# Expert weights of a Mamba-MLA decoder: the gate-up loads move from SyncE's DMA queue to ScalarE's

## Chip, cores and metric

One core of one Trainium2 chip. The metric is the device time of one launch in microseconds (us). The kernel before took 1404.7 us, the median of three runs that went from 1397.98 to 1405.53 us.

## The reference, cut to what matters

The model is a trunk of two layers, one step on 256 prompt rows and 64 sample rows (320 rows of 1024 numbers, float32). Layer 0 mixes tokens with a state-space scan, layer 1 with latent attention. Each mixer is followed by a mixture of experts, and this is the part that the change touches:

```python
def hier_moe(x, router, router_bias, w_gate, w_up, w_down):
    ...
    # every row picks one group of 8 experts, then 2 experts in it; gate = their weights
    for g in range(MOE_GROUPS):
        hg = silu(einsum('nd,edf->nef', xt, w_gate[sl])) * einsum('nd,edf->nef', xt, w_up[sl])
        hg = hg * gate[:, sl, None]
        out = out + einsum('nef,efd->nd', hg, w_down[sl])
```

There are 32 experts in a layer. One expert has a gate and an up matrix of 1024 x 256 and a down matrix of 256 x 1024: 2 MB of gate-up weights and 1 MB of down weights, some 100 MB in a layer. All of it is read from HBM once per layer.

## The kernel before, in words

`expert_layer(layer, afterwards)` (line 827) is called twice, after the scan and after the attention. Experts are worked on in 16 **pairs** (j = 0 to 15; pair j is experts 2j and 2j+1). Each expert has 64 places for rows, so that a pair fills the 128 partitions. The loop over windows (`Fori(0, n_windows)`) runs once here: no expert has more than 64 rows.

**Slots.** The weights of six experts lie in SBUF at a time: `slot(i)` is slot i % 6, four of them in `ring` and two in `hi`. A slot holds gate-up weights (16 KB in each partition) and behind them down weights (8 KB in each partition). So the loads of pair j go where pair j-3 was.

**TensorE** (lines 1131 to 1143) runs `gate_up(j+1)`, then `turn_hidden(j)`, `turn(j+2)`, `down(j)`. `gate_up` (L1098, 32 matmuls) waits for its gate-up loads; it makes gate and up outputs of both experts and raises `gu_done`. `turn_hidden` and `turn` are transposes (L1110, L1083); `down` (L1125, 16 matmuls) waits for its down loads and raises `d_done`. `idle_work` (L1024) is a pair of matmuls whose output nobody reads.

**ScalarE** (lines 1187 to 1197) runs, for each j, `silu(j+1)` (L1178, waits for `gu_done` of j+2), `rows_in(j+2)` (L1172, four activations behind `turn(j+2)`, which `gate_up(j+2)` waits for) and `rows_out(j)` (L1184, behind `down(j)`). Before the change it issues no weight load.

**SyncE** issues all weight loads on its own DMA queue, in an order written out by hand. The first six experts are issued ahead of the loop. Experts 6 and 7 (pair 3) are issued in halves (L219) as pair 0 is used. Then `stream(sp, 4, PAIRS + 1)` (lines 978 to 988) does for each j: wait until `gate_up(j-3)` has read its slots, issue the gate-up loads of pair j (L211, two DMAs); wait until `down(j-4)` is done, issue the down loads of pair j-1 (L224, two DMAs). Within one queue a later DMA's packets stand behind an earlier one's.

**GpSimd** gathers the input rows of pair j+3 (L1222, an indirect DMA) and scatters the output rows of pair j (L1230), on a third queue.

In the profile the queues have numbers: q1 is SyncE's, q10 ScalarE's, q0 GpSimd's. ScalarE's queue is used before the change for three loads at the end of each expert layer alone (L1205), beside three of SyncE (L1008).

Of the kernel before, what the change touches and what calls it, by code (L numbers as in the profile page):

```python
# [53 lines left out]
PAIRS = EXPERTS // 2  # L54
# [87 lines left out]
def program(nc, a, o):  # L142
    ctx = ExitStack()
    with ctx:
# [64 lines left out]
        def load_gate_up(sp, layer, i, slot):  # L209

            sp.dma_start(slot[:, 0:2 * KD * FF],  # L211
                         a["experts"][layer * EXPERTS + i][:, 0:2 * KD * FF]).then_inc(gate_up_in[i % RING], 16)

        def load_half_gate_up(sp, layer, i, slot, half):

            def part(x):
                return x.rearrange("p (g k f) -> p g k f", g=2, k=KD)[:, :, half * KD // 2:(half + 1) * KD // 2, :]

            sp.dma_start(part(slot[:, 0:2 * KD * FF]),  # L219
                         part(a["experts"][layer * EXPERTS + i][:, 0:2 * KD * FF])).then_inc(gate_up_in[i % RING], 16)  # L220

        def load_down(sp, layer, i, slot):

            sp.dma_start(slot[:, 2 * KD * FF:WEXP],  # L224
                         a["experts"][layer * EXPERTS + i][:, 2 * KD * FF:WEXP]).then_inc(down_in[i % RING], 16)

        def first_expert(sp, layer, i, slot=None):

            slot = ring[:, i, :] if slot is None else slot
            load_gate_up(sp, layer, i, slot)  # L230
            load_down(sp, layer, i, slot)
# [595 lines left out]
        def expert_layer(layer, afterwards):  # L827


            with ExitStack() as st:  # L830
# [39 lines left out]
                def slot(i):  # L870
                    return ring[:, i % RING, :] if i % RING < 4 else hi[:, i % RING - 4, :]
# [24 lines left out]
                def load_windows(eng):  # L896
                    eng.wait_ge(windows_set, 1)
                    return eng.value_load(windows[0:1, 0:1], min_val=1, max_val=MAX_WINDOWS)

                def meet(eng, w):  # L900

                    eng.wait_ge(go, w + 1)
                    eng.sem_inc(passed, 1)
# [65 lines left out]
                @block.sync  # L969
                def _(sp):  # L970
                    for t in range(NT):
                        sp.wait_ge(norm_set, t + 1)
                        sp.dma_start(x_dram[OFF[t]:OFF[t] + ROWS[t], :], X[0:ROWS[t], t, :]).then_inc(x_out, 16)
                    for i in (4, 5):
                        first_expert(sp, layer, i, slot(i))
                    n_windows = sp.alloc_register(f"windows_sp{layer}")
                    with sp.Fori(0, n_windows) as w:
                        def stream(sp, first, last):

                            for j in range(first, last):  # L980
                                if j < PAIRS:
                                    sp.wait_ge(gu_done, j - 2)
                                    for i in (2 * j, 2 * j + 1):
                                        load_gate_up(sp, layer, i, slot(i))
                                if j > 3:
                                    sp.wait_ge(d_done, j - 3)
                                    for i in (2 * j - 2, 2 * j - 1):
                                        load_down(sp, layer, i, slot(i))

                        for half in range(2):  # L990
                            sp.wait_ge(gu_done if half else half_done, 1)
                            for i in (6, 7):
                                load_half_gate_up(sp, layer, i, slot(i), half)
                        with sp.If(w < 1):
                            sp.wait_ge(x_scaled, 1)
                            sp.dma_start(lnp[:, :, :], a["ln"][2 * layer + 1]).then_inc(ln_in, 16)
                        stream(sp, 4, PAIRS + 1)
                        sp.wait_ge(d_done, PAIRS)
                        found = load_windows(sp)
                        sp.reg_mov(n_windows, found)  # L1000
                        sp.sem_inc(arrived, 1)
                        meet(sp, w)
                        with sp.If(w + 1 < found):
                            for i in range(RING):
                                first_expert(sp, layer, i, slot(i))
                    for t in range(NT):
                        r, row = ROWS[t], TOK + OFF[t]
                        sp.dma_start(places[NT + t][0:r, :], y_dram[row:row + r, :]).then_inc(got_in[NT + t], 16)  # L1008
                    if afterwards:
                        for got in got_in:  # L1010
                            sp.wait_ge(got, 16)
                        afterwards(sp)
                    else:
                        for t in range(NT):
                            sp.wait_ge(norm_set, NT + t + 1)
                            sp.dma_start(o["y"][0:ROWS[t], t, :], X[0:ROWS[t], t, :]).then_inc(stored, 16)
                        sp.wait_ge(stored, 16 * NT)
# [139 lines left out]
                @block.scalar  # L1157
                def _(act):
                    columns_in(act, 0)
                    statistics(act, 0)  # L1160
                    act.activation(spare[:, :], eps[:, 0:1], ACT.Sigmoid)
                    for t in range(NT):
                        flipped_act(act, 0, t)
                    act.wait_ge(logit_done, 2)
                    act.activation(aff[:, 0:2, :], ps[:, LG[0], 0:64].rearrange("p (t e) -> p t e", t=2), ACT.Sigmoid)
                    act.wait_ge(logit_done, 3)
                    act.activation(aff[0:64, 2, :], ps[0:64, LG[2], 64:96], ACT.Sigmoid).then_inc(aff_done, 1)

                    def rows_in(j):
                        act.wait_ge(turned, 2 * j + 1)  # L1170
                        for k in range(EARLY):
                            ins = act.activation(xsT[:, j % 2, k, :], ps[:, TP[0], k * P:(k + 1) * P], ACT.Identity,  # L1172
                                                 bias=gb[:, 0, 1, k:k + 1], scale=gb[:, 0, 0, k:k + 1])
                        ins.then_inc(xs_act, 1)

                    def silu(j):
                        act.wait_ge(gu_done, j + 1)
                        act.activation(sg[:, j % 2, :], ps[:, GU[j % 2], 0:FF], ACT.Silu).then_inc(silu_done, 1)  # L1178

                    def rows_out(w, j):  # L1180
                        act.wait_ge(d_done, j + 1)
                        if j >= 2:
                            act.wait_ge(ys_out[j % 2], PER_WINDOW * w + 16 * (j // 2))
                        act.activation(ys[:, j % 2, 0:512], ps[:, YB[0], :], ACT.Copy).then_inc(y_act, 1)  # L1184

                    n_windows = act.alloc_register(f"windows_act{layer}")
                    with act.Fori(0, n_windows) as w:
                        act.activation(spare[:, :], eps[:, 0:1], ACT.Silu)
                        rows_in(0)
                        silu(0)  # L1190
                        rows_in(1)
                        for j in range(PAIRS):
                            if j + 1 < PAIRS:
                                silu(j + 1)
                            if j + 2 < PAIRS:
                                rows_in(j + 2)
                            rows_out(w, j)
                        act.reg_mov(n_windows, load_windows(act))
                        act.wait_ge(y_act, PAIRS)
                        act.sem_inc(arrived, 1)  # L1200
                        meet(act, w)

                    for t in range(NT):
                        r, row = ROWS[t], OFF[t]
                        act.dma_start(places[t][0:r, :], y_dram[row:row + r, :]).then_inc(got_in[t], 16)  # L1205
                    act.activation(spare[:, :], eps[:, 0:1], ACT.Sqrt)
                    if layer == 0:
                        columns_in(act, 1)
                    statistics(act, 1)
                    if layer == 0:  # L1210
                        for t in range(NT):
                            flipped_act(act, 1, t)
# [986 lines left out]
```

## Time and profile before

| | |
|---|---|
| median of the runs | 1404.7 us |
| the profiled execution's own time | 1403.22 us |
| its span, first to last instruction | 1401.5 us |
| mean granted TensorE clock | 0.87 of full speed |
| TensorE matmuls busy | 1204.4 us, 86% of the span |
| ScalarE busy | 223.4 us, 16% |
| DMA traffic | 309.33 MB, mean 221 GB/s |
| share of SyncE's queue | 293.32 MB in 39666 packets |

The profile is of one execution. A line such as `L1098 PE MATMUL` is a group of instructions of one source line; "x32" is how many. In the timeline the bracket at a line's end says how long the engine was idle before and what ended it. A DMA engine is one of 16 that all queues of the core share; a "packet" of the profile is what such an engine moves in one piece. "DMA share" is how busy the 16 engines were on average; it can read a little above 1 because neighbouring packets overlap.

### The profile page before, as it was taken

What the parts mean: (1) busy time and instruction counts of PE and PEld (TensorE: products, weight loads), DVE (VectorE), ACT (ScalarE), POOL (GpSimd) and SP (SyncE); (2) the same over time, 40 slices, a digit from 0 to 9 for tenths busy, and PEclk for the clock granted to TensorE, in tenths of its full rate; (3) what the DMA queues carried; (4) which work ended last, traced back from release to release, by engine and by line L of the source; (5) the groups of instructions that cost most, each with busy time, mean ns of one, the idle gap of its engine ahead of it and who ended that gap; (6) DMA issues with size and microseconds to landing.
All of it is one profiled execution on the core that took longest, in us unless ns stands there. A gap on an engine that the chain in (4) does not pass through costs nothing. (4 is left out here: it accounts for less than half of the span.)

```text
span 1401.5 us, 14254 instructions
## 1 busy us (share of the span) xinstructions
PE 1204.4 (86%) x5008; PEld 641.1 (46%) x5008; DVE 442.5 (32%) x1137; ACT 223.4 (16%) x521; POOL 158.7 (11%) x231
## 2 busy tenths in 40 slices
PE   6999966676999699989999884889989989998981
PEld 4777754555566333543333323455554543333330
DVE  0037755543433410451212116222210362121115
ACT  0101121211000200311211112132120311111112
POOL 0000002423000000011111100314000011111100
PEclk9999987665555799899999996899999889999996
DMA  5333450000242224669999957535620869999973
GB/s 225 127 127 126 190 229 21 1 31 1 90 145 94 109 90 180 246 229 415 421 423 424 424 240 302 172 114 162 230 106 15 344 238 408 424 424 422 425 311 123
DMA packets 51726, 309.33 MB, mean 221 GB/s; under 512 B 12818, under 2 KB 13714, under 8 KB 30290
## 3 DMA queue, kind: packets, MB, share of 16 engines
q1 hardware_dynamic: 39666, 293.32, 52.5%
q0 software_dynamic: 11264, 12.61, 2.7%
q10 hardware_dynamic: 736, 2.62, 0.6%
q8 instruction: 35, 0.57, 0.2%
q14 instruction: 25, 0.20, 0.0%
HBM read 300.61 MB, written 30.97 MB: 237 GB/s over the span
## 5 line engine op out<-in xcount | busy, mean ns | idle before, releaser
L1098 PE MATMUL ps<-ring,xsT 128*64 128x512 f32 x704 | 166.7, 628 | 22.5 <-DMA ring<-in_experts 18.0
L302 PE MATMUL ps<-XT,ring 128*128 128x320 f32 x640 | 174.6, 436 | 11.3 <-DMA ring<-in_w_in 11.3
L302 PEld LDWEIGHTS ps<-XT,ring 128*128 128x128 f32 x640 | 122.7, 192 | 62.7 <-issue 12.7
L1098 PEld LDWEIGHTS ps<-ring,xsT 128*64 128x64 f32 x704 | 56.8, 144 | 129.4 <-issue 122.9
L1420 DVE TENSOR_TENSOR work<-work,ps 128x256 f32<-128x256 f32 x32 | 13.4, 420 | 272.2 <-ACT work L1178 272.2
L822 PE MATMUL ps<-ring,zT 128*128 128x512 f32 (+1 forms) x192 | 87.8, 605 | 0.0
L1125 PE MATMUL ps<-ring,hT 128*64 128x512 f32 x352 | 80.4, 598 | 2.2 <-DVE hT L1425 1.7
L1098 PE MATMUL ps<-hi,xsT 128*64 128x512 f32 x320 | 74.2, 618 | 7.5 <-DMA hi<-in_experts 7.3
L1230 POOL DMA_INDIRECT y_dram<-ys,index x32 | 32.1, 1004 | 378.1 <-DVE ys L1431 367.1
L1222 POOL DMA_INDIRECT XT<-x_dram,index x32 | 32.7, 1023 | 357.6 <-DVE index L1366 325.8
L1024 PE MATMUL ps<-C 128*128 128x512 f32 x124 | 70.6, 688 | 0.0
L721 PE MATMUL ps<-ring,Bm 64*128 64x512 f32 x64 | 57.5, 1077 | 0.0
L1178 ACT ACTIVATE work<-ps 128x256 f32<-128x256 f32 x32 | 12.3, 385 | 279.0 <-PE ps L1098 279.0
L822 PEld LDWEIGHTS ps<-ring,zT 128*128 128x128 f32 (+1 forms) x192 | 30.5, 172 | 56.8 <-issue 56.6
L530 PE MATMUL ps<-seg,ring 128*64 128x128 f32 (+1 forms) x192 | 22.3, 356 | 39.1 <-DVE seg L589 39.1
L1172 ACT ACTIVATE xsT<-ps,gb 128x128 f32<-128x128 f32 x128 | 48.2, 457 | 45.5 <-PE ps L1083 45.5
L1275 DVE SCALAR_TENSOR_TENSOR X<-X,ps 128x1024 f32<-128x1024 f32 (+1 forms) x6 | 7.3, 1211 | 137.5 <-PEq L759 79.1
L1098 PEld LDWEIGHTS ps<-hi,xsT 128*64 128x64 f32 x320 | 24.5, 142 | 56.2 <-issue 56.2
L1431 DVE COPY ys<-ps 128x512 f32<-128x512 f32 x32 | 22.1, 692 | 81.3 <-PE ps L1125 81.3
L1413 DVE TENSOR_SCALAR xsT<-ps,gb 128x128 f32<-128x128 f32 x128 | 43.7, 403 | 11.4 <-PE ps L1083 9.6
L1953 PE MATMUL ps<-ring,XT 128*128 128x512 f32 (+1 forms) x96 | 44.4, 605 | 0.0
L1125 PEld LDWEIGHTS ps<-ring,hT 128*64 128x64 f32 x352 | 23.3, 136 | 45.2 <-issue 37.7
(290 smaller groups left out, 1514.4 us busy)
## 6 DMA issues: line engine op xcount, KB each, us to landing
ring<-in_experts SPq DMA_DIRECT2D x40, 2048.0 KB, 27.4
ring<-in_experts SPq DMA_DIRECT2D x52, 1024.0 KB, 26.0
hi<-in_experts SPq DMA_DIRECT2D x20, 2048.0 KB, 27.2
ring<-in_w_in SPq DMA_DIRECT2D x10, 2048.0 KB, 7.8
hi<-in_experts SPq DMA_DIRECT2D x20, 1024.0 KB, 32.5
ring<-in_latent SPq DMA_DIRECT2D x60, 256.0 KB, 4.2
ring<-in_w_out SPq DMA_DIRECT2D x4, 2048.0 KB, 12.3
ring<-in_state SPq DMA_DIRECT2D x4, 1024.0 KB, 6.9
```

The costliest lines, as they stand in the source:

```text
L302: mm = pe.matmul(ps[:, q, 0:TOK], ring[:, u, k * 512 + q * P:k * 512 + (q + 1) * P], XT[:, k, :], start=(k == 0), stop=(k == KD - 1))
L530: mm = pe.matmul(out, xdt[0:r, h * HP:(h + 1) * HP], seg[0:r, u % 2, j, 0:r], start=True, stop=not carried)
L721: pe.matmul(ps[:, UP[g], :], Bm[:, b % 2, g * STATE:(g + 1) * STATE], xdtw[0:64, g * 512:(g + 1) * 512], start=True, stop=True).then_inc(u ...
L822: mm = pe.matmul(ps[0:ROWS[t], 2 * t + n, :], zT[:, blk, OFF[t]:OFF[t] + ROWS[t]], ring[:, blk // 4, at:at + 512], start=(blk == 0), stop= ...
L1024: pe.matmul(ps[:, bank, :], ident, C[:, 0:512], start=True, stop=True)
L1098: mm = pe.matmul(ps[e * SLOTS:(e + 1) * SLOTS, GU[p], :].rearrange("p (g f) -> p g f", g=2), xsT[:, p, k, e * SLOTS:(e + 1) * SLOTS], w[:, ...
L1125: mm = pe.matmul(ps[e * SLOTS:(e + 1) * SLOTS, YB[m], :], hT[:, p, f, e * SLOTS:(e + 1) * SLOTS], slot(2 * j + e)[:, at:at + 512], start=( ...
L1172: ins = act.activation(xsT[:, j % 2, k, :], ps[:, TP[0], k * P:(k + 1) * P], ACT.Identity, bias=gb[:, 0, 1, k:k + 1], scale=gb[:, 0, 0, k: ...
L1222: pool.indirect_dma_start(out=xs[:, j % 2, :], out_offset=None, in_=x_dram, in_offset=bass.IndirectOffsetOnAxis(ap=index[:, 0, j:j + 1], a ...
L1230: pool.indirect_dma_start(out=y_dram, out_offset=bass.IndirectOffsetOnAxis(ap=index[:, 1, j:j + 1], axis=0), in_=ys[:, j % 2, :], in_offse ...
L1413: ins = v.tensor_scalar(xsT[:, j % 2, k, :], ps[:, TP[k // 4], k % 4 * P:(k % 4 + 1) * P], gb[:, 0, 0, k:k + 1], gb[:, 0, 1, k:k + 1], ALU ...
L1953: mm = pe.matmul(ps[0:ROWS[t], 2 * t + n, :], XT[:, h, OFF[t]:OFF[t] + ROWS[t]], w_o(h)[:, n * 512:(n + 1) * 512], start=(h == 0), stop=(h ...
```

## The change

Pairs 4 to 15 lose their gate-up loads in SyncE's `stream`. ScalarE issues them instead, right behind `silu(j+1)`, which waits on the same count of `gu_done` as SyncE did. SyncE keeps the down loads with their wait, and all loads of pairs 0 to 3.

```diff
--- before.py
+++ after.py
@@ stream, on SyncE
                             for j in range(first, last):
-                                if j < PAIRS:
-                                    sp.wait_ge(gu_done, j - 2)
-                                    for i in (2 * j, 2 * j + 1):
-                                        load_gate_up(sp, layer, i, slot(i))
                                 if j > 3:
                                     sp.wait_ge(d_done, j - 3)
                                     for i in (2 * j - 2, 2 * j - 1):
                                         load_down(sp, layer, i, slot(i))
@@ on ScalarE
+                    def reload(j):
+                        if 4 <= j < PAIRS:
+                            for i in (2 * j, 2 * j + 1):
+                                load_gate_up(act, layer, i, slot(i))
+
@@
                         for j in range(PAIRS):
                             if j + 1 < PAIRS:
                                 silu(j + 1)
+                                reload(j + 4)
                             if j + 2 < PAIRS:
                                 rows_in(j + 2)
                             rows_out(w, j)
```

## Rows read from the trace of the kernel before

**Rows 1.** The page, chain that ended last, by line.

```profile
DMA ring<-in_experts 8%; PE ps L1098 5%; PE ps L1125 2%; DMA hi<-y_dram 1%; PE ps L1037 1%; PE ps L1083 0%; PE ps L1024 0%; DVE X L1482 0%; DVE X L1485 0%; ACT xsT L927 0%; DMA XT<-x_dram,index 0%; ACT xsT L1172 0%; DMA y_dram<-ys,index 0%; DVE X L1469 0%; PE ps L1110 0%
```

**Rows 2.** Busy time by windows, expert pairs of layer 1.

```profile
core 0: us, PE busy (x) PEld busy (x) DVE busy (x) ACT busy (x) POOL busy (x), PEclk, DMA share, GB/s
1160.00:1340.00 180.00, 167.70 (x756) 61.42 (x756) 36.59 (x91) 32.37 (x78) 25.36 (x25) 0.97 1.01 421
```

**Rows 3.** The same view, expert pairs of layer 0.

```profile
622.00:810.00 188.00, 175.36 (x786) 64.43 (x784) 36.58 (x91) 32.36 (x78) 25.33 (x25) 0.97 1.01 421
```

**Rows 4.** Timeline of TensorE, layer 1: start us, us, operation, idle before.

```profile
1244.01 7.09 PE L1098 MATMUL ps<-hi,xsT 128*64 128x512 f32 x32
...
1258.73 7.09 PE L1098 MATMUL ps<-ring,xsT 128*64 128x512 f32 x32 [1.65 <-DMA ring<-in_experts]
...
1330.03 1.04 PE L1083 MATMUL ps<-C,XT 128*128 128x128 f32 x8
...
1338.77 8.78 PE L1098 MATMUL ps<-hi,xsT 128*64 128x512 f32 x32 [2.96 <-DMA hi<-in_experts]
...
1354.10 7.09 PE L1098 MATMUL ps<-ring,xsT 128*64 128x512 f32 x32 [0.57 <-DMA ring<-in_experts]
...
1367.32 3.65 PE L1125 MATMUL ps<-ring,hT 128*64 128x512 f32 x16 [0.84 <-DVE hT L1425]
```

**Rows 5.** Timeline of TensorE, layer 0: gate-ups of pairs 9, 12 and 15.

```profile
727.57 7.09 PE L1098 MATMUL ps<-ring,xsT 128*64 128x512 f32 x32 [2.09 <-DMA ring<-in_experts]
...
775.51 8.78 PE L1098 MATMUL ps<-ring,xsT 128*64 128x512 f32 x32 [2.71 <-DMA ring<-in_experts]
...
822.92 7.09 PE L1098 MATMUL ps<-ring,xsT 128*64 128x512 f32 x32 [0.64 <-DMA ring<-in_experts]
```

**Rows 6.** Chain that ended last, in order of time: load of pair 15.

```profile
1317.24 36.62 DMA ring<-in_experts
```

**Rows 7.** Busy time by windows of 2 us, end of the loads in layer 1.

```profile
1352.00:1354.00 2.00, 1.53 (x6) 0.30 (x2) 0.69 (x1) 0.60 (x1) 0.00 (x1) 1.00 0.65 274
...
1362.00:1364.00 2.00, 1.55 (x8) 0.63 (x10) 0.40 (x2) 0.00 (x0) 0.00 (x0) 1.00 0.25 102
1364.00:1366.00 2.00, 2.00 (x10) 0.43 (x6) 0.00 (x0) 0.00 (x0) 0.00 (x0) 1.00 0.00 0
```

**Rows 8.** Timeline of SyncE, layer 1: DMA issues, L211 gate-up, L224 down.

```profile
1160.14 0.82 SPq L211 DMA_DIRECT2D ring<-in_experts  x2
1165.07 0.97 SPq L224 DMA_DIRECT2D ring<-in_experts  x2
...
1270.78 5.31 SPq L224 DMA_DIRECT2D hi<-in_experts  x2
...
1334.80 0.80 SPq L224 DMA_DIRECT2D ring<-in_experts  x2
```

**Rows 9.** DMA view of the stretch 1160 to 1340 us.

```profile
DMA packets 10053, 75.72 MB, mean 421 GB/s; under 512 B 3239, under 2 KB 3239, under 8 KB 4221
...
q1 hardware_dynamic: 6589, 71.71, 94.8%
...
ring<-in_experts SPq DMA_DIRECT2D x16, 2048.0 KB, 31.8
...
XT<-x_dram,index POOLq DMA_INDIRECT x12, 13.4
```

**Rows 10.** Timeline of ScalarE behind the gate-up of pair 8.

```profile
1251.14 0.39 ACT L1178 ACTIVATE work<-ps 128x256 f32<-128x256 f32 x1 [7.40 <-PE ps L1098]
1251.94 1.51 ACT L1172 ACTIVATE xsT<-ps,gb 128x128 f32<-128x128 f32 x4 [0.41 <-PE ps L1083]
```

**Rows 11.** DMA view, 1378 to 1382 us: both queues loading 4 KB rows.

```profile
q1 hardware_dynamic: 230, 0.88, 54.0%
q10 hardware_dynamic: 200, 0.75, 47.5%
```

**Rows 12.** Timeline of GpSimd: the gather of pair 14.

```profile
1305.81 1.02 POOL L1222 DMA_INDIRECT XT<-x_dram,index  x1 [0.30 <-issue]
```

**Rows 13.** Timeline of ScalarE: its DMA issues at the layer's end.

```profile
1375.72 1.34 ACTq L1205 DMA_DIRECT2D hi<-y_dram  x3
```

## The prediction

> **What bounds the kernel now.** I read the chain of waits first. Its largest share is the load of expert weights, 8% of the span, and the chain as written covers layer 1's expert stage alone [rows 1]. Next I read the windows: over the expert pairs the 16 DMA engines are busy all the time and move 421 GB/s, in layer 1 [rows 2] and in layer 0 alike [rows 3]. So both expert stages are held by the stream of weights. The timeline of TensorE says from when. Up to pair 8 its gate-up starts without a wait; from pair 9 on it waits for its weights (1.65 us at pair 9, 2.96 at pair 14, 0.57 at pair 15) [rows 4], and layer 0 looks the same [rows 5]. The reader should see a pattern here: with one pair every 13 us from TensorE (period between 1244.01 and 1258.73 less the wait of 1.65) [rows 4] and 4.19 + 2.10 MB of weights per pair at 421 GB/s, 14.9 us, TensorE is the faster one and runs into the loads.
>
> Then the order matters. The total of bytes is fixed, and the loads end at about 1364 us whatever stands first: DMA share is 0.25 up to 1364 and 0.00 behind it [rows 7]. The gate-up of pair 15 starts at 1354.10, when its own load landed (issued 1317.24, 36.62 us on the way) [rows 6, 4]. So 10 us of loads come behind it: the down weights of pairs 14 and 15, 4.19 MB at 421 GB/s = 10.0 us. TensorE needs them only behind gate-up 15 and two transposes, the last one at 1367.32 [rows 4]; that they come late costs nothing. What counts for the end of each stage is **when the gate-up load of pair 15 lands**, and the single queue serves it ahead of two pairs of down weights.
>
> **The change, part by part.**
> Removed from SyncE, 24 issues in each layer and 12 waits: two issues take 0.82 us [rows 8]. SyncE computes nothing, and the engines have work queued, so this gives 0. The issue even took 5.31 us for two at 1270.78 [rows 8], while the queue was deep; nobody waited for it. SyncE's down issues are no longer behind a gate-up issue, but their wait on `down` comes later than the gate-up wait anyway: 0.
>
> Added on ScalarE, 24 issues in each layer. They stand between `silu` and `rows_in`. Price: three of ScalarE's own issues took 1.34 us [rows 13], so two take 0.9. Behind them is `rows_in`: it started 0.80 us after `silu` started [rows 10]; now it starts 0.39 + 0.9 = 1.3 us after. It ends then at 2.8 us, and the next gate-up comes 5.9 us after the last one ended (13.0 less 7.09), so there are 3 us of cover. From below, 0; from above, if the issue blocks as SyncE's did (5.31), `rows_in` is late by 1.2 us, in a stretch where TensorE waits up to 3 us for weights anyway: still 0. I take 0. Each queue now also holds half of the DMAs, which speaks against such a block.
>
> The issue itself comes one `silu` later, 0.4 us [rows 10]. Where the engines have a backlog that is nothing; at pair 4, first of the stream, there is hardly one, so the whole stream ends 0.4 us later in each layer. Between 0 and 0.8.
>
> **The order** is the large term. Two queues now hold the loads, and the engines have to divide themselves between them. In the stretch 10053 less 4221 packets are of 8 KB and over, and SyncE's queue moved 71.71 MB: 12.3 KB each, the mean of 16 and 8 KB [rows 9]. So a packet is one partition's row: 16 KB of gate-up or 8 KB of down weights, and each pair brings every engine 16 of one and 16 of the other. At 421/16 GB/s they take 0.62 and 0.31 us. Where both queues were in use with equal packets, they moved 230 and 200 in 4 us [rows 11]: turn by turn, roughly. If packets take turns here, the gate-up queue gets two thirds of the bytes, just what it brings, and neither queue runs away from the other. Gate-up keeps the lead of its first issue: 1160.14 against 1165.07 [rows 8], 4.93 us, 8 packets. When the 192nd and last gate-up packet of an engine is served (12 pairs of 16), 184 of the 208 down packets (13 pairs) are: 24 are left, 7.4 us. Today 32 are left, 9.9 us. The gate-up load of pair 15 lands 2.5 us later. From below: turns that favour ScalarE's queue, so that more is left; the bound is the rival of the other side. From above: all down weights in before it, 9.9 us. I take 2.5, since it rests on the nearest row, and note that it is sensitive: a tilt of 5% in the turns is 9 packets, 2.8 us.
>
> **TensorE's clock.** A gate-up after a wait of 2.71 us took 8.78 us, 1.7 more, and one after 2.09 us took 7.09 [rows 5]. The granted clock of that stretch is 0.97 in the mean [rows 2]. Slowed pairs are hidden behind the next load, except pair 15. Slow and full pairs alternate today: 14 slow after 2.96, 15 full after 0.57 [rows 4]. When all landings move by 2.9 us, the first long wait moves from pair 10 to pair 9 and the alternation turns over: pair 14 full, then pair 15 waits 1354.10 - 1338.77 - 13.0 = 2.3 us, between the row that was slowed and the one that was not. I charge 1.7 once, not twice; 0 to 3.4 in all.
>
> Sum: 2 x (2.5 + 0.4) + 1.7 = 7.5 us on the profiled execution's 1403.2 (1.5 below the median of 1404.7): **1411 us**, if it is right with 1406 to 1417 as this case's own range.
>
> **A page beside the rows.** Here the rows say that packets of 8 and 16 KB take turns. The Trainium skill, DMA: Bandwidth & Descriptors, section "SWDGE vs HWDGE vs iDMA", puts the boundary at which an engine changes queues at preferably 4096 B; by that, the queues would share bytes and the last gate-up load would come behind nearly all down weights. It is the first rival. Its overview, Trainium Kernel Development and Optimization, section Key Constraints, says that issuing from several engines only saves issue time; by that the time would be today's, the second rival.
>
> **Rivals.**
> *Equal bytes, or turns tilted to SyncE* (slower by more). Down then gets half, needs 10 us for a pair that comes every 15, and is always done early; the load of pair 15 is the last to land, 9.9 us later. 2 x (9.9 + 0.4) + 1.7 = 22 us: 1425, up to 1429 with both clocks slowed. For it: 200 against 230 packets for ScalarE's queue [rows 11]. Against: that window holds the start of both, and the packet sizes of rows 9. Between this case and mine there is a continuum.
> *Order kept* (the descriptors go to the engines in order of issue, or the backlog is shorter than it looks): only 0.4 us per layer, 1404. For it: the loads come out of one set of 16 engines. Against: rows 11, and a gather of GpSimd, issued into a backlog in which a 2 MB load took 31.8 us, landed in 13.4 [rows 9].
> *ScalarE's queue wins* (faster). If the turns favour gate-up, its last load lands earlier and the down weights become the last thing. Place: down of pair 15, which now starts at 1367.32 and can't start before the last byte lands, about 1364.1: 3.2 us per layer at most, 6.4 in all: 1397. It decides from 184 gate-up against 176 down packets, a tilt of 5% to ScalarE. Rows 11 lean the other way.
> *A third queue starves the gathers.* A gather takes 13.4 us among one queue [rows 9]; behind two, with 0.93 us instead of 0.46 per turn, some 20. The gather of pair 14 was issued at 1305.81 [rows 12] and read at 1330.03 [rows 4], 24 us. It fits; if it didn't, TensorE would lose 2 to 3 us in one or two late pairs: 1413 to 1416.
>
> **How the numbers follow.** Mine 0.50, equal bytes or a tilt that way 0.24, order kept 0.14, ScalarE wins 0.06, gathers 0.06. A measurement of this kernel can tell about 0.5%, 7 us. My case lies at the bound: a little over half of it counts as slower. With the rival of 22 us and the gathers that makes slower 0.56. No change takes the rest of my case, the order kept and most of the faster one: 0.38. Faster 0.06. The range goes from 1401 (order kept, with the spread of the runs) to 1427 (equal bytes).
>
> **What would show it.** In the changed profile the rows L211 stand on ScalarE's queue, q10, with some 100 MB. The DMA share stays at 1.0 and the loads end where they did, within 1 us. TensorE's first wait for weights comes at pair 8 or 9 and is 3 us longer in total; the gate-up of pair 15 starts about 2.9 us later against the first gate-up of its layer. If it starts 10 us later, the equal bytes hold; if not later, the order was kept. Gate-up loads take longer from issue to landing, down loads shorter. `rows_in` starts 0.5 us later and nobody waits. I am wrong altogether if TensorE's waits fall on ScalarE or on a gather, or if the DMA rate changes from 421 GB/s.

## The result, and the profile after

The changed kernel took 1428.41 us (median of 4 runs, 1427.56 to 1435.43) beside 1404.1 us before: ratio 1.0193, 95% interval 1.0156 to 1.023. It is **slower by 24 us**, 12 in each expert layer. The forecast was 1411 with a range up to 1427; the direction was right, the size was not.

The page of the changed kernel, first the queues, then the chain that ended last by line, then the matmuls of `gate_up` and the transposes that read the gathered rows. L1079, L1094 and L1121 are the old L1083, L1098 and L1125.

```profile
q1 hardware_dynamic: 32754, 192.65, 35.0%
q10 hardware_dynamic: 7648, 103.29, 17.4%
...
DMA XT<-x_dram,index 10%; PE ps L1121 3%; PE ps L1094 2%; PE ps L1079 1%; PE ps L1033 1%; DMA hi<-y_dram 0%; POOL y_dram L1232 0%; DVE ys L1433 0%; DVE X L1484 0%; DVE X L1487 0%; ACT xsT L927 0%; ACT xsT L1168 0%; DMA y_dram<-ys,index 0%; DVE X L1471 0%; DVE X L1467 0%
...
L1094 PE MATMUL ps<-ring,xsT 128*64 128x512 f32 x704 | 155.9, 595 | 4.8 <-ACT xsT L1168 4.8
...
L1079 PE MATMUL ps<-C,XT 128*128 128x128 f32 x256 | 40.3, 308 | 43.8 <-DMA XT<-x_dram,index 43.7
```

The change did what its text says: q10 moved 103.29 MB, where it had 2.62 before. But the chain's largest part is no longer a load of weights, as in [rows 1]; it is `XT<-x_dram,index`, GpSimd's gather of the input rows. `gate_up` doesn't wait for weights once; the transposes of `turn` wait for gathers, 43.7 us in all. A chain's share (10%) is time spent in flight, not time lost.

Waits of TensorE in layer 1 of the changed kernel (us in total, times, longest), and then its DMA view for the expert stage (count, KB, median us from issue to landing):

```profile
PE ps L1079 <- DMA XT<-x_dram,index: 21.8, 10, 2.9
```

```profile
ring<-in_experts ACTq DMA_DIRECT2D x16, 2048.0 KB, 18.8
...
XT<-x_dram,index POOLq DMA_INDIRECT x15, 22.4
y_dram<-ys,index POOLq DMA_INDIRECT x14, 16.0
```

A gather takes 22.4 us where it took 13.4 [rows 9]. The weights now come early: 18.8 us from issue to landing for 31.8 [rows 9]. That is no faster DMA, it is a shorter backlog, since TensorE asks for them later.

The timeline of TensorE in layer 1, some pairs (start us, us, idle before):

```profile
1153.92 7.09 PE L1094 MATMUL ps<-ring,xsT 128*64 128x512 f32 x32 [1.51 <-ACT xsT L1168]
...
1198.65 1.09 PE L1079 MATMUL ps<-C,XT 128*128 128x128 f32 x8 [1.43 <-DMA XT<-x_dram,index]
...
1214.71 1.09 PE L1079 MATMUL ps<-C,XT 128*128 128x128 f32 x8 [2.94 <-DMA XT<-x_dram,index]
...
1270.17 7.09 PE L1094 MATMUL ps<-hi,xsT 128*64 128x512 f32 x32
...
1326.65 1.97 PE L1079 MATMUL ps<-C,XT 128*128 128x128 f32 x8 [2.92 <-DMA XT<-x_dram,index]
1328.55 5.64 PE L1121 MATMUL ps<-ring,hT 128*64 128x512 f32 x16
...
1358.63 1.09 PE L1079 MATMUL ps<-C,XT 128*128 128x128 f32 x8 [2.86 <-DMA XT<-x_dram,index]
...
1378.99 7.09 PE L1094 MATMUL ps<-ring,xsT 128*64 128x512 f32 x32
```

The waits in the loop begin at 1198.65, at the turn of pair 4, where the kernel before ran without any. From the first gate-up to the last (1153.92 to 1378.99) it is 225.1 us. I use this distance below for each run: before it was 211.4 us in layer 0 and 212.4 in layer 1, after it is 223.7 and 225.1. That is 25.0 us more in all, the whole of the loss. Behind five of the six waits of 2.6 to 2.9 us in layer 1 the matmuls are slow, now those of `down` and sometimes of `turn` (5.64 us for 3.65 behind the wait of 2.92), but not behind the one at 1214.71.

### The profile page after: what moved, and what is told of

It is laid out like the page before. It is cut to its first block and busy times, and to the rows that moved or that the text cites. A ratio compares the mean times of both kernels' runs of the same rounds, so it can differ in the third digit from the quotient of the medians.

```text
span 1425.8 us, 14254 instructions
## 1 busy us (share of the span) xinstructions
PE 1212.2 (85%) x5008; PEld 639.2 (45%) x5008; DVE 441.2 (31%) x1137; ACT 223.3 (16%) x521; POOL 158.6 (11%) x231
## 2 busy tenths in 40 slices
DMA packets 51726, 309.33 MB, mean 217 GB/s; under 512 B 12818, under 2 KB 13714, under 8 KB 30290
## 3 DMA queue, kind: packets, MB, share of 16 engines
q10 hardware_dynamic: 7648, 103.29, 17.4%
## 5 line engine op out<-in xcount | busy, mean ns | idle before, releaser
L1094 PE MATMUL ps<-ring,xsT 128*64 128x512 f32 x704 | 155.9, 595 | 4.8 <-ACT xsT L1168 4.8
L302 PEld LDWEIGHTS ps<-XT,ring 128*128 128x128 f32 x640 | 122.6, 192 | 62.7 <-issue 12.7
L1094 PEld LDWEIGHTS ps<-ring,xsT 128*64 128x64 f32 x704 | 50.3, 137 | 106.8 <-issue 100.0
L1121 PE MATMUL ps<-ring,hT 128*64 128x512 f32 x352 | 92.3, 672 | 1.9 <-DVE hT L1427 1.7
L1422 DVE TENSOR_TENSOR work<-work,ps 128x256 f32<-128x256 f32 x32 | 13.4, 420 | 232.5 <-ACT work L1174 232.5
L1079 PE MATMUL ps<-C,XT 128*128 128x128 f32 x256 | 40.3, 308 | 43.8 <-DMA XT<-x_dram,index 43.7
L1094 PE MATMUL ps<-hi,xsT 128*64 128x512 f32 x320 | 70.9, 595 | 0.0
L1415 DVE TENSOR_SCALAR xsT<-ps,gb 128x128 f32<-128x128 f32 x128 | 43.7, 403 | 63.8 <-PE ps L1079 63.4
L1079 PEld LDWEIGHTS ps<-C,XT 128*128 128x128 f32 x256 | 32.2, 157 | 52.2 <-DMA XT<-x_dram,index 50.5
L1121 PEld LDWEIGHTS ps<-ring,hT 128*64 128x64 f32 x352 | 26.1, 153 | 53.6 <-issue 49.8
L1174 ACT ACTIVATE work<-ps 128x256 f32<-128x256 f32 x32 | 12.3, 384 | 238.9 <-PE ps L1094 238.9
## 6 DMA issues: line engine op xcount, KB each, us to landing
ring<-in_experts ACTq DMA_DIRECT2D x32, 2048.0 KB, 18.8
```

Source lines behind the costliest of these rows:

```text
L302: mm = pe.matmul(ps[:, q, 0:TOK], ring[:, u, k * 512 + q * P:k * 512 + (q + 1) * P], XT[:, k, :], start=(k == 0), stop=(k == KD - 1))
L1079: tr = pe.transpose(ps[:, TP[half], k * P:(k + 1) * P], xs[:, p, at:at + P], ident)
L1094: mm = pe.matmul(ps[e * SLOTS:(e + 1) * SLOTS, GU[p], :].rearrange("p (g f) -> p g f", g=2), xsT[:, p, k, e * SLOTS:(e + 1) * SLOTS], w[:, ...
L1121: mm = pe.matmul(ps[e * SLOTS:(e + 1) * SLOTS, YB[m], :], hT[:, p, f, e * SLOTS:(e + 1) * SLOTS], slot(2 * j + e)[:, at:at + 512], start=( ...
L1415: ins = v.tensor_scalar(xsT[:, j % 2, k, :], ps[:, TP[k // 4], k % 4 * P:(k % 4 + 1) * P], gb[:, 0, 0, k:k + 1], gb[:, 0, 1, k:k + 1], ALU ...
```

## Why 22 us are too many

Three theories stood to be told apart. **Theory 1**: a gather lands too late beside two weight queues. **Theory 2**: the order of the weights, with equal bytes for both queues. **Theory 3**: the issue on ScalarE's own queue delays `rows_in`.

How do the engines divide themselves? First the counts of packets. DMA view of 1230 to 1330 us, the changed kernel:

```profile
q10 hardware_dynamic: 1827, 26.66, 63.2%
q1 hardware_dynamic: 1834, 13.35, 31.8%
q0 software_dynamic: 1844, 2.05, 5.7%
```

The same stretch before:

```profile
q1 hardware_dynamic: 3664, 40.15, 95.1%
q0 software_dynamic: 1820, 2.04, 5.8%
```

Three queues, and each moved the same number of packets, though the bytes go 13 to 7 to 1. By itself this says only what was asked for: each queue brings 18 packets per pair to each engine (16 rows of weights and two closing packets of 4 B, or 8 rows and one closing packet for the scatter and for the gather each), and the one queue before brought 36. What shows the turns is the order. The trace lists the start and the length of every packet, but not its engine; if each is put behind a packet that ended just then, a packet of q0 is followed by one of q1 in 76% of the cases, one of q1 by q10 in 65%, one of q10 by q0 in 65% (no order at all would give a third). So packets take turns one by one, a row of 16 KB as one of 4 B, as the forecast had it for two queues. (The Trainium skill, DMA: Bandwidth & Descriptors, section "Queues, rings and completion order", has each DMA engine go round its queues packet by packet. The trace agrees, with one row as the packet. The 4096 B of the skill's section "SWDGE vs HWDGE vs iDMA" on the same page don't fit this trace: rows of 16384 B went as one turn each.)

Behind one weight queue each packet of the gather waits for one weight packet, 0.46 us in the mean; behind two, for one of each, 0.93. The scatter of the output rows stands ahead of the gather in the same queue. A gather on idle engines takes 3.3 us; with 18 turns for scatter and gather an estimate is 3.3 + 18 x 0.52 = 12.7 before and 3.3 + 18 x 0.98 = 20.9 after (0.05 for its own packet, the mean of q0 above), against 13.4 and 22.4 measured.

And the slack was smaller than I had it. In the kernel before, in the stretch where TensorE ran free, the gather was issued at 1219.96 and read at 1238.30. GpSimd's and then TensorE's timeline of the kernel before:

```profile
1219.96 1.02 POOL L1222 DMA_INDIRECT XT<-x_dram,index  x1 [0.30 <-issue]
```

```profile
1238.30 1.04 PE L1083 MATMUL ps<-C,XT 128*128 128x128 f32 x8
...
1274.78 8.78 PE L1098 MATMUL ps<-ring,xsT 128*64 128x512 f32 x32 [2.98 <-DMA ring<-in_experts]
```

The slack is 1238.30 - 1219.96 = 18.3 us. Since the gather of pair j+4 is issued only behind the scatter of pair j, gather, turn, down and scatter form a ring over two pairs: 22.4 + 1.0 + 3.65 and 2.85 from the end of `down` to the next gather, 29.9 us, and up to 3 more where `turn` and `down` are slow. What it gives is (1358.63 - 1198.65) / 10 = 16.0 us per pair from the turn of pair 4 to that of pair 14, where TensorE needs 13.0.

This 16.0 is not a number of the ring alone. The kernel before goes at the same pace once it waits for weights: the gate-up of pair 10 started at 1274.78, that of pair 14 at 1338.77 [rows 4], 16.0 per pair. And the engines are as full in the changed kernel as they were [rows 2]; its windows, in the columns of [rows 2]:

```profile
1200.00:1350.00 150.00, 133.21 (x566) 46.75 (x564) 27.16 (x68) 23.83 (x58) 19.28 (x19) 0.93 1.01 419
```

So 16.0 us is what the engines take for the bytes of a pair. Before, a gather landed within its slack, and TensorE ran ahead at 13.0 up to pair 8, on weights that were there. With two weight queues it is held to the engines' pace by the gathers from pair 4 on. The gate-up of pair 8 starts 116.3 us after the first one (1270.17 - 1153.92), where it was 102.3 (1244.01 [rows 4] - 1141.71); from there to the last one it is 108.8, where it was 110.1. The loss is made by pair 8 and never won back, while the weights lie ready.

## The experiments

All are compared with the kernel before on the same chip.

**Gathers earlier.** `e1` is the changed kernel, `e2` the kernel before, each with

```diff
-                        for j in range(3):
+                        for j in range(4):
                             gather(j)
                         for j in range(PAIRS):
-                            if j + 3 < PAIRS:
-                                gather(j + 3)
+                            if j + 4 < PAIRS:
+                                gather(j + 4)
                             scatter(j)
```

> The changed kernel with each gather of GpSimd issued ahead of the scatter of the pair four before it, some 6 us earlier, and no longer behind that scatter in the queue. Theory 1 (the gathers land too late behind two weight queues: 22.4 us instead of 13.4, and TensorE waits for them at turn, 43.7 us in all): the waits at turn go, TensorE waits for weights again, and the time is that of the weights' order, 1404 to 1412 us; gathers may still take 15 to 22 us. Theory 2 (the order of the weights: the last gate-up load lands up to 10 us late per layer): still 1422 to 1428 us, now with waits for weights. Theory 3 (the issue on ScalarE between silu and rows_in delays the gate-ups): 1428 us, unchanged.

> The kernel before with the same earlier gathers. All theories: no more than 1 us of wait for gathers is there to be saved (1.6 us in the whole profile), so 1401 to 1406 us. It is the control for what the earlier gather does by itself.

Measured: e1 1409.43 us, ratio 1.0055 (1.0039 to 1.007); e2 1404.0 us, 1.0025 (1.0009 to 1.0041). Of 24 us, 5.4 are left against e2. By the distances more is left: from first to last gate-up e1 takes 214.0 and 218.2 us, e2 211.2 and 210.3, 10.7 us in the two layers of 25.0; the first gate-up of each layer came some 5 us earlier in e1 than in e2, and why is open. This is for theory 1 and against 2 and 3: the order of the weights and ScalarE's issues are the same as in the changed kernel. But the waits did not go, against what I expected. Waits of TensorE, the landing times and two pieces of the chain that ended last in e1:

```profile
PE ps L1079 <- DMA XT<-x_dram,index: 37.1, 18, 2.9
```

```profile
ring<-in_experts ACTq DMA_DIRECT2D x16, 2048.0 KB, 30.0
...
XT<-x_dram,index POOLq DMA_INDIRECT x12, 29.8
```

```profile
1255.82 29.77 DMA XT<-x_dram,index
1287.00 30.64 DMA XT<-x_dram,index
```

The gathers became slower still, 29.8 us, because GpSimd's queue now has a backlog of its own. All three queues bring 18 packets per pair to each engine and in turns advance together: over 1260 to 1330 us 82% of the packets of each queue are followed by one of the next. The ring is shorter (no `down`, no scatter), the gathers are longer by as much, and the pace is again 16.0 us: (1349.70 - 1253.58) / 6 between the turns of pairs 9 and 15. A gather's length is thus no fixed cost; what the earlier issue gains is that TensorE falls to the engines' pace at pair 8, not at pair 4. The chain in e1 still runs over gathers and not over weights, so that e1 is not the case of the forecast. A sum of waits, 37.1 here against 43.7 in the changed kernel, didn't tell how much time it cost.

**One queue again, on ScalarE; and the two queues changed over.** `e3` keeps the change and takes the down loads out of `stream` and to ScalarE too, which leaves `stream` empty; `e4` is the kernel before with only the down loads moved. Both have on ScalarE:

```diff
                             rows_out(w, j)
+                            if 3 <= j + 3 < PAIRS:
+                                for i in (2 * j + 6, 2 * j + 7):
+                                    load_down(act, layer, i, slot(i))
```

> All loads of the stream on ScalarE's one queue, in the old order: gate-up behind silu, down behind rows_out; SyncE issues none of them. Theory 1: one weight queue again, gathers back at about 13.4 us, no waits at turn, 1403 to 1406 us. Theory 2: order as before, so also 1403 to 1406. Theory 3: ScalarE issues 48 instead of 24 DMAs per layer in its stream, so 1428 us or more.

> The queues changed over: gate-up stays with SyncE, the down loads go to ScalarE behind rows_out. Theory 1: two weight queues, gathers at 22 us, 1425 to 1431 us as in the changed kernel. Theory 2: the same if the turns are equal. Theory 3: nothing stands between silu and rows_in any more, so 1404 us.

Measured: e3 1401.91 us, ratio 0.9994 (0.9978 to 1.001); e4 1427.1 us, 1.018 (1.015 to 1.021). Theory 3 is out twice: ScalarE can issue all 50 loads of a layer's stream (24 of gate-up and 26 of down weights), two in up to 4.4 us, and costs nothing; and with nothing between `silu` and `rows_in`, the loss is there. What counts is the number of queues, not the engine that issues. The landing times of e4:

```profile
XT<-x_dram,index POOLq DMA_INDIRECT x14, 23.0
```

and of e3:

```profile
XT<-x_dram,index POOLq DMA_INDIRECT x13, 13.6
```

**The order by itself.** `e5` (changed kernel) and `e6` (before) leave out the gathers from pair 2 on:

```diff
                     def gather(j):
                         if j >= 2:
-                            pool.wait_ge(turned, 2 * (j - 1))
+                            return
...
-                        pe.wait_ge(xs_in[p], PER_WINDOW * w + 16 * (j // 2) + 16)
+                        if j < 2:
+                            pe.wait_ge(xs_in[p], PER_WINDOW * w + 16)
```

> The changed kernel with the gathers of pairs 2 to 15 left out: those pairs work on the rows of pairs 0 and 1, with the same matmuls. Nothing can wait for a gather any more; what is left of the loss against e6 is the order of the weights. Theory 1 with packets taking turns one by one: the last gate-up load lands 2.5 to 3 us late per layer, so 5 to 9 us above e6, with waits for weights. Theory 2 (equal bytes, all down weights in first): 20 us above e6. Order without any effect: 0 to 1 us above e6.

> The kernel before with the same gathers left out, the control for e5. The engines that carry the gathered rows have some 9 us less to do per layer, so the loads end earlier: 1385 to 1400 us by all theories.

Measured: e5 1393.75 us, ratio 0.9928 (0.9903 to 0.9952); e6 1388.63, 0.989 (0.9864 to 0.9917): 5.1 us between them, with four executions of each and intervals that touch. Without gathers the change costs 5.1 us, with them 24. Both wait for weights. The last gate-up of layer 1, e5 and then e6:

```profile
1138.12 7.09 PE L1095 MATMUL ps<-ring,xsT 128*64 128x512 f32 x32 [1.51 <-ACT xsT L1169]
...
1343.45 8.78 PE L1095 MATMUL ps<-ring,xsT 128*64 128x512 f32 x32 [2.30 <-DMA ring<-in_experts]
```

```profile
1138.25 7.09 PE L1099 MATMUL ps<-ring,xsT 128*64 128x512 f32 x32 [1.51 <-ACT xsT L1173]
...
1340.34 8.78 PE L1099 MATMUL ps<-ring,xsT 128*64 128x512 f32 x32 [2.34 <-DMA ring<-in_experts]
```

205.3 us from first to last gate-up against 202.1; in layer 0 it is 205.3 against 202.9. So the new order costs about 3.2 and 2.5 us, from one profile each; the forecast's term was 2.5 + 0.4. How far such a distance moves by itself, the kernels with one weight queue and all gathers say (before, e2, e3, e8): 211.2 to 211.4 in layer 0, 210.3 to 212.4 in layer 1. The term is clear of that in layer 0, and hardly in layer 1. Equal bytes (20 us) is out.

**The size of a turn.** `e7` wrote each row as two pieces in the changed kernel:

```diff
-            sp.dma_start(slot[:, 0:2 * KD * FF],
-                         a["experts"][layer * EXPERTS + i][:, 0:2 * KD * FF]).then_inc(gate_up_in[i % RING], 16)
+            sp.dma_start(slot[:, 0:2 * KD * FF].rearrange("p (c f) -> p c f", c=2),
+                         a["experts"][layer * EXPERTS + i][:, 0:2 * KD * FF].rearrange("p (c f) -> p c f", c=2)
+                         ).then_inc(gate_up_in[i % RING], 16)
...
```

> The changed kernel with each 16 KB row of gate-up weights written as two pieces of 8 KB and each 8 KB row of down weights as two of 4 KB. If the pieces become packets, a turn of the two weight queues takes half the time. Theory 1 (a packet of the third queue waits for one packet of each weight queue): gathers fall from 22 us to 12 to 15, the waits at turn go, 1408 to 1413 us. If a gather's time doesn't depend on turns but on bandwidth: 22 us and 1425 to 1431. If the pieces are merged, all is as in the changed kernel.

Measured 1427.03 us, and 51726 packets as before: the pieces were merged, and the run says nothing on turns. `e9` (kernel before) and `e10` (changed kernel) use the helper of pair 3, whose rows of 4 KB can't be merged:

```diff
-                                        load_gate_up(sp, layer, i, slot(i))
+                                        for half in range(2):
+                                            load_half_gate_up(sp, layer, i, slot(i), half)
...
-                            halves = 16 if i >= 6 and i % RING < 2 else 0
-                            pe.wait_ge(gate_up_in[i % RING], 16 * (i // RING) + 16 + halves)
+                            pe.wait_ge(gate_up_in[i % RING], 32 * (i // RING) + 16)
```

> The kernel before with each gate-up load of pairs 4 to 15 issued as two DMAs with rows of 4 KB in place of one with rows of 16 KB; still one weight queue. Turns (a packet of GpSimd's queue waits for one weight packet): a turn beside gate-up takes 0.16 us instead of 0.62, so a gather, 13.4 us, takes 8 to 10. By bandwidth alone it would stay at 13.4. The time: 1400 to 1412, since weights bind and small rows may move a few per cent slower (408 against 421 GB/s).

> The same in the changed kernel. Turns: a turn of all three queues takes 0.16 + 0.31 us, half of before, so gathers fall from 22.4 to 11 to 14 us and the waits at turn (43.7 us) go. But the down weights now get 8 KB for each 4 KB of gate-up and are all in first, so the last gate-up load lands up to 10 us late per layer: 1418 to 1428 us, all waits for weights. If gathers are held by bandwidth and not by turns: 22 us, waits at turn, 1428.

Measured: e9 1414.28 us, ratio 1.009 (1.0055 to 1.0125); e10 1436.61 us, 1.0243 (1.0207 to 1.0279). The gathers of e9 and then of e10:

```profile
XT<-x_dram,index POOLq DMA_INDIRECT x13, 8.2
```

```profile
XT<-x_dram,index POOLq DMA_INDIRECT x15, 8.8
```

With the same bytes to move and smaller packets, a gather falls from 13.4 to 8.2 us (the estimate with 18 turns gives 7.6), and in the changed kernel from 22.4 to 8.8: turns it is, not bandwidth. In e10 the estimate gives 12.7, and 11 to 14 were expected, so it is too high there; over 1250 to 1330 us, where the engines had work nearly all the time, a gather took 11.0. The times miss on the high side. e9 probably pays for its small rows: 410 GB/s over 1250 to 1330 us, where the kernel before moved 423. e10 I had wrong: no waits for weights, but 63.1 us for ScalarE, and ScalarE's timeline says why:

```profile
1268.07 0.39 ACT L1173 ACTIVATE work<-ps 128x256 f32<-128x256 f32 x1 [6.70 <-PE ps L1093]
1268.07 13.22 ACTq L219 DMA_DIRECT2D ring<-in_experts  x4
1281.35 1.51 ACT L1167 ACTIVATE xsT<-ps,gb 128x128 f32<-128x128 f32 x4 [12.89 <-issue]
```

Four issues took 13.22 us, and `rows_in` stood behind them. Theory 3's mechanism exists, but not in the changed kernel: there two issues took 0.82 to 0.99 us in layer 1. That the many small packets in the queue are the reason is likely, not shown.

**Which pairs cost.** `e11` is the changed kernel with ScalarE issuing pairs 4 to 8 and SyncE the rest. `e12` is the reverse, with the two conditions exchanged (`j < 9` on SyncE, `9 <= j < PAIRS` on ScalarE):

```diff
                             for j in range(first, last):
+                                if 9 <= j < PAIRS:
+                                    sp.wait_ge(gu_done, j - 2)
+                                    for i in (2 * j, 2 * j + 1):
+                                        load_gate_up(sp, layer, i, slot(i))
...
-                        if 4 <= j < PAIRS:
+                        if 4 <= j < 9:
```

> ScalarE issues the gate-up loads of pairs 4 to 8 alone, SyncE those of 9 to 15 in the old order. If a wait for a gather costs wherever it falls, about 5 twelfths of the loss stay: 1413 us. If it costs only from where the weights would have bound (pair 9 on), the early waits are swallowed: 1402 to 1406 us.

> The other half: SyncE pairs 4 to 8, ScalarE 9 to 15. If every wait costs alike, about 7 twelfths stay: 1417 us. If the late ones are what counts: 1415 to 1428 us; the more of the loss is here, the more the end of the stream decides.

Measured: e11 1404.74 us, ratio 1.0013 (0.9998 to 1.0028); e12 1419.81 us, 1.0124 (1.0091 to 1.0157). Waits of TensorE in e11, and its last gate-up:

```profile
PE ps L1083 <- DMA XT<-x_dram,index: 17.5, 9, 4.2
```

```profile
1355.27 7.09 PE L1098 MATMUL ps<-ring,xsT 128*64 128x512 f32 x32 [2.29 <-DMA ring<-in_experts]
```

In e11 TensorE still waits 17.5 us for gathers, and none of it shows: the distance from first to last gate-up is 211.1 and 210.3 us, no longer than before, and the last one waits for weights again. At the gate-up of pair 8 e11 was 9.3 us behind (111.6 us after the first one, for 102.3) the kernel before; with one weight queue from pair 9 on it ran at 13.0 us per pair until it met the weights. The early waits only use up the lead that the weights take back from pair 9 on. The loss needs gathers that stay late to the end. e12 brings a loss of its own besides:

```profile
1264.53 9.38 PE L1098 MATMUL ps<-hi,xsT 128*64 128x512 f32 x32 [11.62 <-DMA hi<-in_experts]
```

Pair 8 waits 11.62 us: its load, issued at 1221.34, stands in SyncE's backlog and takes 42.94 us; pair 9's, issued at 1233.98 on the empty queue of ScalarE, take 20.0 and pass it. So e12 doesn't measure the late waits alone.

**Something to gain.** `e8` is the kernel before with the load of the norm's parameters moved behind the stream:

```diff
-                        with sp.If(w < 1):
-                            sp.wait_ge(x_scaled, 1)
-                            sp.dma_start(lnp[:, :, :], a["ln"][2 * layer + 1]).then_inc(ln_in, 16)
                         stream(sp, 4, PAIRS + 1)
+                        with sp.If(w < 1):
+                            sp.wait_ge(x_scaled, 1)
+                            sp.dma_start(lnp[:, :, :], a["ln"][2 * layer + 1]).then_inc(ln_in, 16)
```

> The kernel before with the load of the norm's parameters (1 MB, L996) issued behind the whole stream of weights instead of ahead of it; it is needed only when the DMA engines are idle again. If the landing of the last gate-up load sets the end of the layer, as the prediction has it, all weights land 1 MB / 421 GB/s = 2.5 us earlier in each layer: 1396 to 1400 us. If something else sets the end, 1403.

Measured 1401.33 us, ratio 0.9994 (0.998 to 1.0007): no difference that can be told. From first to last gate-up it was 211.3 us in layer 0, as before, and 210.3 in layer 1, 2.1 less. But e3, which doesn't touch this load, has 210.9 there, so that much comes and goes between runs, and a gain isn't shown, though 1396 to 1400 were expected; where the 2.5 us went is open. No version here beats the kernel before.

## Why the prediction was wrong, point by point

- **What bounds the kernel**: right. The weights' stream, and within it the landing of the last gate-up load. e11 shows it best: 17.5 us of other waits vanish in it. Two readings in it were off. The 14.9 us per pair gave the weights all of the 421 GB/s, though gathers and scatters share the engines; 16.0 were measured. And of the 4.19 MB said to come behind the last gate-up load, 2.1 MB did: the windows of 2 us from 1354 to 1364 show 293, 254, 223, 197 and 102 GB/s. The engines don't finish together, and the 10 us hold for the last of them alone.
- **SyncE's part, and the issues on ScalarE at nothing**: right. e3 and e4 show it.
- **The order**, 2.5 + 0.4 us per layer: right in mechanism, and in size as far as can be told. Packets take turns one by one, and e5 less e6 gives 3.2 and 2.5 us per layer, 5.1 us in the time, not far above what runs differ by. The term for TensorE's clock, 1.7 once, isn't shown apart: the last gate-up was slow in e5 and in e6 alike.
- **The rival of equal bytes**, to which I gave 0.24: its time (1425) came near the result, its mechanism did not happen. Who had seen only the total would have taken it for confirmed.
- **The step that failed is the rival of the gathers.** The mechanism was named and the latency not far off ("some 20", measured 22.4). Two things in it were wrong. "It fits" compared it with 24 us between issue at 1305.81 [rows 12] and turn at 1330.03 [rows 4], in a stretch where TensorE was already waiting for weights, so that the slack had been stretched by the very wait. Where TensorE ran free it was 18.3 us, less than my own 20. And the price, "2 to 3 us in one or two late pairs", took it for a single delay. It comes back at nearly every pair from 4 on: TensorE goes at 16.0 us per pair, where it had gone at 13.0 up to pair 8, and the gathers replaced the weights as what it waits for. With the order's part that makes 12.3 and 12.7 us per layer, where the rival had 2 to 5 in all. A chance of 0.06 for it was far too little.
- **The sum** thus lacked its largest term. That e1 came to 1409.43, near the 1411 of the forecast, confirms nothing: TensorE waits for gathers there too.
- **What would show it**: "wrong altogether if TensorE's waits fall on a gather" is what came. The first wait came at the turn of pair 4, not at pair 8 or 9.

What stays open: in e1 the rest of 5.4 us over e2 (10.7 by the distances) may be the order's term, the gathers' or both; its waits are recorded at gathers, and no run takes the two apart there.

## To carry to other kernels

A load that moves to another queue changes not only who issues it, but how many turns everybody else's packets wait: count the packets per turn for the small, latency-bound transfers on the remaining queues, above all an indirect gather of many rows. Measure the slack of a prefetch where the consumer runs free; where it waits for something else, the slack is lent. And when a wait grows, look for the ring of dependences that it closes, since a ring can be paid at each round and a single delay once. A delay counts only if the consumer can't catch up later: compare the distances over the first and the second half of the stage, not the sums of waits.

## What the runs showed of the hardware

Three queues with packets of 16 KB, 8 KB and mostly 4 KB or 4 B take turns packet by packet: in e1 82% of the packets of each queue are followed by one of the next. A queue of some 2 MB per 100 us takes as many turns as one of 27 MB (1844 and 1827 in the changed kernel) and can build a backlog of its own (gathers of 29.8 us in e1). A DMA issue can hold its engine: 13.22 us for four issues of 4 KB rows on ScalarE in e10, up to 4.4 us for two in e3, against 0.8 us for two in most places. A contiguous row written as two pieces was moved as one packet (e7).
